# Spatial gate of the two late layers moved between the q and k projections and done in place, and the state output put back in channel order by ACT

## The chip, the cores and the metric

The kernel runs on one core of a Trainium2 chip. Its time is the device time of one execution in microseconds (us); the median of three runs of the kernel before is 2917.49 us (2912.63 to 2918.08). The engines are PE (TensorE, matmuls and transposes), DVE (VectorE), ACT (ScalarE), POOL (GpSimd) and SP (SyncE, which here only issues transfers). Each has its own instruction queue and works it off in order; they meet at semaphores.

## What is computed

The reference is a model of four layers at 512 tokens and width 1024, all in f32: an attention layer and a convolution layer with a mixture of experts, and then two "late" layers that this change is about. What a late layer does before its feed-forward part, cut to what matters:

```
def spatial_gating(u, v, v_gain, w_s, b_s):        # 256 channels, windows of 128 positions, 4 heads
    v = rms_norm_2(v, v_gain).reshape(bsz, nwin, GMLP_WINDOW, GMLP_HEADS, GMLP_HEAD_DIM)
    w = jnp.where(mask[None], w_s, 0)
    mixed = jnp.einsum("hij,bnjhc->bnihc", w, v) + b_s.T[None, None, :, :, None]
    return u * mixed.reshape(bsz, seq, GMLP_WIDTH)

xn = rms_norm_2(h, attn_norm_g[layer])
u_ssm, u_g, v_g, q, k, v = jnp.split(xn @ w_in[layer], [o1, o2, o3, o4, o5], axis=-1)
y_ssm = s5_mixer(u_ssm, ...)                       # complex diagonal state space model, 256 channels
y_sgu = spatial_gating(u_g, v_g, ...)
y_diff = diff_attention(q, k, v, ...)              # 4 heads, two softmax maps each, their difference on v
mixed = jnp.concatenate([y_ssm, y_sgu, y_diff], axis=-1)
h = h + mixed @ w_out[layer]
```

## The kernel before

The program is written by hand for each engine, and nothing is scheduled by a tool: what stands in a block (`block.tensor`, `block.vector`, `block.scalar`, `block.gpsimd`) runs in that order. Large products are done in three f32r matmuls per tile (L598 to L600: high times high, low times high, high times low), for which POOL splits each weight tile in two (L2024 rounds, L2026 takes the rest). PSUM has eight banks and every PE result takes the next one in turn (`claim`): a tile can begin only when the tile eight places before it was drained.

A late layer `l` (0 or 1; the code loops over `L2`) has these stages on PE.

- **In-projection.** u for the state space model (names `u`), then the 512 columns of the gate, `ugv` (u_g and v_g, token-major, 4 tiles), then the 512 columns of v, `vD`. ACT takes both out of PSUM (L1879). Then ACT computes the root mean square of v_g (L1883 to L1885), copies the turned gate weights (`wT`, L1887), and works out the exponentials of lambda.
- **The q/k stage.** `normed(groups2(l), ...)` runs over eight groups, q and k of head 0, q and k of head 1, and so on. In step i PE does the projection of group i (24 matmuls), the mean square of group i-1 (L800) and the rotation of group i-2 (L814). `between(i, end)` puts attention work between the groups from step 4 on.
- **The tail.** The last units of attention, the state space model and the gate, up to the out-projection `out2`. Attention has 16 units m = 4 x head + query tile. `attend(i)` does the scores of unit i+2 (PE L1287, DVE `maxima` L2918), the exponentials (ACT `probs` L1896), the ratio of the two maps (DVE L2926, L2927), its application (ACT L1905), the merging of the maps (POOL L2331), and for units i and i-1 the turning of the probabilities (PE L1295, ACT L1914) and their product with v (PE L1305, ACT `take_values` L1923, L1924). The state space model runs in two halves a: `state_in` (PE L1260), `turn_in` (DVE L2881), `scan` (DVE L2895), `turn_out` (DVE L2904 to L2907), `state_out` (PE L1271, L1274).

In the tail, before this change: `vn`, the normalised v_g, is written by DVE (L2978) after the last rotation, since its place in the arena is also that of a buffer of the rotations. PE multiplies it by the turned weights in `spatial_gate` (L1247), after `attend(7)`. DVE adds the bias and multiplies by u_g into `gate_out` (L2988) after `scan(0)`. `take_runs(a)` (DVE L2970) copies the state output of half a (key `yp`) from runs of 32 partitions back into channel order, in 16 copies of 32 partitions x 128 elements, each to columns 4 apart, after `attend(10)` and `attend(14)`. `TURN_AFTER` says after which `attend` PE turns the finished tiles of the out-projection's input (`turn_tile(k)`, L1327: k = 2, 3 the gate, 4 to 7 the heads); ACT rounds them (`round_late`, L1946) and DVE takes the rest (`rest_late`, L2945), after the same unit and after the next. POOL splits the first weights of `out2` two units at a time after `merge_maps(13)`, `(14)` and `(15)`.

Of the kernel before, what the change touches and what calls it, by code (L numbers as in the profile page):

```python
# [11 lines left out]
ALU = mybir.AluOpType  # L12
# [35 lines left out]
TURN_AFTER = {10: (4,), 11: (2, 3), 12: (5,), 15: (6,)}  # L48
# [88 lines left out]
def build(nc, A, out, upto=99):  # L137
    ctx = ExitStack()
    with ctx:
# [127 lines left out]
        gate_out = region(18688, 2, T)  # L267
# [28 lines left out]
        vn = region(21760, NT, 256)  # L296
# [247 lines left out]
        def _(pe):  # L544
# [680 lines left out]
            for l in range(L2):  # L1225
# [92 lines left out]
                def turn_tile(k):  # L1318

                    if k >= 4:  # L1320
                        pe.wait_ge(S("subln_done"), 4 * l + k - 3)
                    else:
                        wait_drained(pe, ("sgu", l, NT - 1))
                    ps = claim(("mt", l, k))
                    for t in range(NT):
                        src = gate_out[:, k - 2, t * P:(t + 1) * P] if k < 4 else qD[:, k - 4, t * P:(t + 1) * P]
                        ins = pe.transpose(ps[:, t * P:(t + 1) * P], src, c("ident"))  # L1327
                    fill(ins, ("mt", l, k))
# [9 lines left out]
                def between(i, end):  # L1338

                    if 4 <= i < 8:  # L1340
                        attend(2 * i - 9)
                    elif i == 8 and end:
                        attend(6)
# [7 lines left out]
                spatial_gate()  # L1351
                attend(8)
                state_in(1)
                attend(9)
                state_out(0)
                for m in range(10, UNITS_LATE + 1):
                    attend(m)
                    for k in TURN_AFTER.get(m, ()):
                        turn_tile(k)
                    if m == 13:  # L1360
                        state_out(1)
# [121 lines left out]
        def _(act):  # L1483
# [388 lines left out]
            for l in range(L2):  # L1872
                (norm_added if l else norm_results)(f"at{l}")
                act.wait_ge(S("rstd_ready"), SPLIT_NORMS.index(f"at{l}") + 1)
                for s, dst in ((f"ugv{l}", ugv), (f"vd{l}", vD)):
                    for t in range(NT):
                        key = ("dn", s, 0, t)
                        ps = wait_filled(act, key)
                        drain(act.activation(dst[:, t, :], ps[:, :], ACT.Copy, scale=rstd[:, t:t + 1]), key)  # L1879
                ln_exp_table()  # L1880
# [4 lines left out]
                act.activation(s5("rstd"), lnv, ACT.Exp, scale=-0.5).then_inc(S("v_rms"), 1)  # L1885
                ps = wait_filled(act, ("wt", l))
# [55 lines left out]

                def round_late(k):

                    ps = wait_filled(act, ("mt", l, k))
                    act.activation(mix_hi[:, k, :], ps[:, :], ACT.Copy).then_inc(S("rows_rounded"), 1)  # L1946
# [11 lines left out]
                for m in range(8, UNITS_LATE + 1):  # L1958
                    attend(m)
                    for k in TURN_AFTER.get(m, ()):  # L1960
                        round_late(k)
# [416 lines left out]
        def _(dve):  # L2378
# [465 lines left out]
            for l in range(L2):  # L2844
# [112 lines left out]
                def between(i, end):  # L2957

                    if 4 <= i < 8:
                        attend(2 * i - 10 + end)  # L2960
                    elif i == 8 and end:
                        attend(6)

                def take_runs(a):

                    key = ("yp", l, a)
                    ps = wait_filled(dve, key)
                    for k in range(4):
                        for s in range(RUN):
                            ins = dve.tensor_copy(yg[32 * k:32 * k + 32, a, s:T:RUN],  # L2970
                                                  ps[32 * s:32 * s + 32, k * P:(k + 1) * P])
                    drain(ins, key)

                normed2(l, rb, between)
                dve.wait_ge(S("v_rms"), l + 1)
                dve.wait_ge(S("rope_done"), 16 + 8 * (l + 1))
                for t in range(NT):
                    dve.scalar_tensor_tensor(out=vn[:, t, :], in0=ugv[:, t, 256:512], scalar=s5("rstd")[:, t:t + 1],  # L2978
                                             in1=vgain, op0=ALU.mult, op1=ALU.mult).then_inc(S("vn_ready"), 1)
                turn_in(0)  # L2980
                attend(7)
                scan(0)
                for t in range(NT):
                    ps = wait_filled(dve, ("sgu", l, t))
                    for h in range(4):
                        hs = slice(h * 64, (h + 1) * 64)
                        at = t * P + (h % 2) * 64
                        ins = dve.scalar_tensor_tensor(out=gate_out[:, h // 2, at:at + 64], in0=ps[:, hs],  # L2988
                                                       scalar=vcol("gmlp_b_s_2", 4 * l + h), in1=ugv[:, t, hs],
                                                       op0=ALU.add, op1=ALU.mult)  # L2990
                    drain(ins, ("sgu", l, t))
# [5 lines left out]
                for m in range(10, UNITS_LATE + 1):  # L2997
                    attend(m)
                    if m == 11:
                        turn_out(1)  # L3000
                    if m in (10, 14):
                        take_runs(m // 4 - 2)
                    for k in TURN_AFTER.get(m - 1, ()):
                        rest_late(k)
# [70 lines left out]
```

## Time and profile before

| | before |
|---|---|
| median of three runs | 2917.49 us |
| the profiled execution | 2922.09 us, of which the span is 2920.3 us |
| PE, DVE, ACT, POOL busy | 96%, 36%, 25%, 53% of the span |
| mean granted TensorE clock | 0.978 |

The span runs from the first to the last recorded instruction of that one execution; 1.8 us lie around it. The profiled execution is 4.6 us above the median. Times in the rows are from the start of the span. The q/k stage of layer 0 is 1755.86 to 1834.30, its tail 1834.30 to 1890.36; in layer 1 the same two are 2367.63 to 2445.99 and 2445.99 to 2502.57. A stage is taken from its first PE instruction to that of the next one.

### The profile page before, as it was taken

The page shows a single profiled execution, that of the slowest core. Times are in us where ns is not written, and L with a number is a line of the kernel's source. Part 1 is how long each engine was busy: PE and PEld are TensorE (multiplying, and loading weights), DVE is VectorE, ACT ScalarE, POOL GpSimd, SP SyncE. Part 2 cuts the span into 40 slices and gives each one's busy share as a digit, 9 for nine tenths or more (in the row PEclk, how much of TensorE's full clock was granted, in tenths as well). Part 3 has the DMA queues.
Part 4 walks back from the last instruction along what each step waited for, and adds up shares of the span by engine and source line. Part 5 has one row for each costly group of instructions (what it writes and reads, how often), then busy time and mean ns, then how long its engine had stood idle before and what let it go on. Part 6 is the DMA issues. An engine that isn't in the chain of part 4 may idle for free.

```text
span 2920.3 us, 38219 instructions
## 1 busy us (share of the span) xinstructions
PE 2803.0 (96%) x14585; PEld 2332.8 (80%) x14585; DVE 1053.3 (36%) x2141; ACT 722.4 (25%) x1799; POOL 1547.1 (53%) x1681
## 2 busy tenths in 40 slices
PE   7899999999999989999999989799999997999999
PEld 3545888888878889999999976678888775788887
DVE  1035652313235510000000233837356327466372
ACT  2135752101120101111111024532112234421020
POOL 2121027777777541322280255468888653588786
PEclk9998999999999979999999999899999998999999
DMA  8460013333253269899999930342332312332321
GB/s 189 101 173 15 16 30 87 97 98 101 83 170 101 59 182 277 246 264 254 258 259 263 274 94 16 120 114 85 110 87 88 100 44 91 101 101 94 101 85 52
DMA packets 540391, 371.25 MB, mean 127 GB/s; under 512 B 31489, under 2 KB 493128, under 8 KB 539307
## 3 DMA queue, kind: packets, MB, share of 16 engines
q1 hardware_dynamic: 522144, 321.58, 39.0%
q0 software_dynamic: 11472, 33.13, 3.6%
q10 hardware_dynamic: 6586, 14.03, 1.9%
q8 instruction: 119, 1.95, 0.3%
q14 instruction: 70, 0.57, 0.1%
HBM read 336.73 MB, written 32.41 MB: 126 GB/s over the span
## 4 chain that ended last, share of the span: by engine, by line
PE 87%; DVE 5%; issue 3%; ACT 2%; DMA 2%; POOL 1%; ACTq 0%; another core or an unknown queue 0%; DVEq 0%; SPq 0%; POOLq 0%
PE bank L598 18%; PE bank L600 18%; PE bank L599 18%; PE bank L758 15%; PE bank L1192 7%; PE bank L852 2%; PE bank L830 2%; DMA ring<-in_ev_w_in 1%; PE bank L840 1%; PE bank L800 1%; PE bank L814 1%; DMA ring<-in_moe_w_up 1%; ACT x_hi L1585 1%; PE bank L957 1%; DVE x L2565 1%
## 5 line engine op out<-in xcount | busy, mean ns | idle before, releaser
L2026 POOL TENSOR_TENSOR unit_parts<-ring,unit_parts 128x512 fp32r<-128x512 f32 x580 | 804.4, 1387 | 48.4
L2024 POOL TENSOR_SCALAR unit_parts<-ring 128x512 fp32r<-128x512 f32 x580 | 423.5, 730 | 488.5 <-PE bank L600 341.1
L598 PE MATMUL bank<-x_hi,unit_parts 128*128 128x512 f32 x1408 | 556.6, 395 | 19.3 <-DVE x L2565 10.3
L599 PE MATMUL bank<-x_lo,unit_parts 128*128 128x512 f32 x1408 | 551.0, 391 | 0.0
L600 PE MATMUL bank<-x_hi,unit_parts 128*128 128x512 f32 x1408 | 551.0, 391 | 0.0
L758 PE MATMUL bank<-arena,ring 128*128 128x160 f32 x2816 | 389.1, 301 | 4.6 <-ACT arena L1771 3.7
L758 PEld LDWEIGHTS bank<-arena,ring 128*128 128x128 f32 x2816 | 386.1, 191 | 5.8 <-ACT arena L1771 3.9
L598 PEld LDWEIGHTS bank<-x_hi,unit_parts 128*128 128x128 f32 x1408 | 266.5, 189 | 78.2 <-issue 11.7
L598 PE MATMUL bank<-unit_parts,hid_parts 128*128 128x512 f32 x784 | 308.3, 393 | 3.2 <-DVE hid_parts L2587 2.6
L599 PEld LDWEIGHTS bank<-x_lo,unit_parts 128*128 128x128 f32 x1408 | 266.2, 189 | 55.9 <-issue 1.4
L600 PEld LDWEIGHTS bank<-x_hi,unit_parts 128*128 128x128 f32 x1408 | 266.1, 189 | 55.9
L600 PE MATMUL bank<-unit_parts,hid_parts 128*128 128x512 f32 x784 | 305.5, 390 | 0.0
L599 PE MATMUL bank<-unit_parts,hid_parts 128*128 128x512 f32 x784 | 305.4, 390 | 0.0
L2633 DVE TENSOR_TENSOR arena<-bank,arena 128x160 f32<-128x160 f32 x88 | 28.6, 325 | 573.6 <-PE bank L758 569.2
L1192 PE MATMUL bank<-arena,ring 128*128 128x160 f32 x1408 | 193.4, 300 | 0.5 <-DVE arena L2633 0.5
L1192 PEld LDWEIGHTS bank<-arena,ring 128*128 128x128 f32 x1408 | 191.5, 190 | 1.0 <-DVE arena L2633 0.7
L1987 ACT ACTIVATE arena<-arena,vec 128x512 f32<-128x512 f32 x88 | 71.9, 817 | 464.4 <-DVE arena L3025 464.4
L2565 DVE TENSOR_TENSOR x<-bank,x 128x512 f32<-128x512 f32 x80 | 55.2, 691 | 335.5 <-PE bank L600 335.5
L598 PEld LDWEIGHTS bank<-unit_parts,hid_parts 128*128 128x128 f32 x784 | 147.5, 188 | 34.9 <-DVE hid_parts L2587 2.8
L600 PEld LDWEIGHTS bank<-unit_parts,hid_parts 128*128 128x128 f32 x784 | 147.3, 188 | 30.8
L599 PEld LDWEIGHTS bank<-unit_parts,hid_parts 128*128 128x128 f32 x784 | 147.4, 188 | 30.5 <-issue 0.5
L3029 DVE SCALAR_TENSOR_TENSOR arena<-arena,vec 128x511 f32<-128x511 f32 x88 | 78.7, 894 | 78.0 <-ACT arena L1987 78.0
(359 smaller groups left out, 3415.5 us busy)
## 6 DMA issues: line engine op xcount, KB each, us to landing
ring<-in_moe_w_gate SPq DMA_DIRECT2D x88, 512.0 KB, 5.9
ring<-in_moe_w_up SPq DMA_DIRECT2D x88, 512.0 KB, 7.1
ring<-in_moe_w_down SPq DMA_DIRECT2D x64, 704.0 KB, 5.0
ring<-in_w_up SPq DMA_DIRECT2D x88, 512.0 KB, 5.2
ring<-in_w_down SPq DMA_DIRECT2D x16, 1024.0 KB, 5.1
ring<-in_od_w_in SPq DMA_DIRECT2D x24, 512.0 KB, 4.6
ring<-in_ffn_w_gate SPq DMA_DIRECT2D x22, 512.0 KB, 4.0
ring<-in_ffn_w_up SPq DMA_DIRECT2D x22, 512.0 KB, 5.2
```

The costliest lines, as they stand in the source:

```text
L598: pe.matmul(ps, a[0], b[0], start=start, stop=False)
L599: pe.matmul(ps, a[0], b[1], start=False, stop=False)
L600: return pe.matmul(ps, a[1], b[0], start=False, stop=stop)
L758: ins = pe.matmul(ps[rows_at:rows_at + m, 0:n], w[:, k * width + at:k * width + at + m], src[:, k, :], start=k == 0, stop=k == KD - 1)
L830: ins = pe.matmul(ps[:, 0:k.shape[1]], u["q"](t), k, start=k is ks[0], stop=k is ks[-1])
L852: ins = pe.matmul(ps[:, 0:u["vw"]], pT_buf[0:w, j % 2, kt * P:kt * P + P], u["v"](kt, w), start=kt == 0, stop=kt == kts - 1)
L1192: ins = pe.matmul(ps[:, (m - m0) * CAP:(m - m0 + 1) * CAP], w[:, k * P:(k + 1) * P], hidE[:, k, :], start=k == 0, stop=k == KE - 1)
L1987: act.activation(acc[:, 2 * a + n % 2, :], unscaled[:, a, :], ACT.Identity, scale=vcol("conv_w_2", 132 * l + 88 + f), bias=vcol("conv_b_2" ...
L2024: pool.tensor_scalar(hi, raw, 1.0, 1.0, ALU.mult, ALU.mult).then_inc(S("units_rounded"), 1)
L2026: pool.tensor_tensor(lo, raw, hi.bitcast(F32), ALU.subtract).then_inc(S("units_split"), 1)
L2565: drain(dve.tensor_tensor(xs, ps[:, :], xs, ALU.add), key)
L3029: link(dve.scalar_tensor_tensor(out=o[:, 1:T], in0=b[:, 0:T - 1], scalar=vcol("conv_w_2", 132 * l + 44 + f), in1=o[:, 1:T], op0=ALU.mult, ...
```

## The change

In both late layers:

- `vn` gets a place in the two ring slots that are held for the attention maps. DVE writes it before the q/k stage and no longer waits for the rotations.
- PE does `spatial_gate` at the end of step 1 of the q/k stage, and DVE its part there too, in place: the product overwrites u_g in `ugv`, and `gate_out` is gone.
- ACT takes `ugv`, computes the root mean square of v_g, and only then takes `vD`.
- `take_runs` goes from DVE to ACT, after the same units.
- `TURN_AFTER`: tiles 2 and 3 are turned after unit 9 instead of 11, tile 4 after unit 11 instead of 10. ACT rounds tile 2 only when tile 3 has been turned too, since it writes where `ugv` stands. `state_out(0)` keeps its place.

```
-TURN_AFTER = {10: (4,), 11: (2, 3), 12: (5,), 15: (6,)}
+TURN_AFTER = {9: (2, 3), 11: (4,), 12: (5,), 15: (6,)}
-        vn = region(21760, NT, 256)
+        vn = held[:, 0:2, :].rearrange("p a (b n) -> p (a b) n", b=2)
 # PE
-                        src = gate_out[:, k - 2, t * P:(t + 1) * P] if k < 4 else qD[:, k - 4, t * P:(t + 1) * P]
+                        src = ugv[:, t, (k - 2) * P:(k - 1) * P] if k < 4 else qD[:, k - 4, t * P:(t + 1) * P]
-                    if 4 <= i < 8:
+                    if i == 1 and end:
+                        spatial_gate()
+                    elif 4 <= i < 8:
...
                 attend(7)
-                spatial_gate()
                 attend(8)
                 state_in(1)
-                attend(9)
-                state_out(0)
-                for m in range(10, UNITS_LATE + 1):
+                for m in range(9, UNITS_LATE + 1):
                     attend(m)
+                    if m == 9:
+                        state_out(0)
 # ACT
+                take_rows(f"ugv{l}", ugv)
                 ln_exp_table()
...
                 act.activation(s5("rstd"), lnv, ACT.Exp, scale=-0.5).then_inc(S("v_rms"), 1)
+                take_rows(f"vd{l}", vD)
...
+                def take_runs(a):
+                    key = ("yp", l, a)
+                    ps = wait_filled(act, key)
+                    for k in range(4):
+                        for s in range(RUN):
+                            ins = act.activation(yg[32 * k:32 * k + 32, a, s:T:RUN],
+                                                 ps[32 * s:32 * s + 32, k * P:(k + 1) * P], ACT.Copy)
+                    drain(ins, key)
                 def round_late(k):
+                    if k == 2:
+                        wait_filled(act, ("mt", l, 3))
...
                     attend(m)
+                    if m in (10, 14):
+                        take_runs(m // 4 - 2)
 # DVE
-                normed2(l, rb, between)
                 dve.wait_ge(S("v_rms"), l + 1)
-                dve.wait_ge(S("rope_done"), 16 + 8 * (l + 1))
                 for t in range(NT):
                     dve.scalar_tensor_tensor(out=vn[:, t, :], in0=ugv[:, t, 256:512], scalar=s5("rstd")[:, t:t + 1],
                                              in1=vgain, op0=ALU.mult, op1=ALU.mult).then_inc(S("vn_ready"), 1)
+                normed2(l, rb, between)
...
-                    if m in (10, 14):
-                        take_runs(m // 4 - 2)
```

The changed file has other line numbers: PE L1246 is before's L1247, L799 is L800, L1286, L1294, L1304 and L1326 are L1287, L1295, L1305 and L1327, L1270 and L1273 are L1271 and L1274; ACT L1900 to L1928 are L1896 to L1924, L1962 is L1946.

PE, layer 0, where the tail begins before: the last rotation (L814), `state_in(0)` (L1260), `attend(7)`, the gate (L1247), and `attend(8)`.

```order
L814 MATMUL bank<-arena,cst 128x512
L1260 MATMUL bank<-arena 128x128 x12
L1287 MATMUL bank<-arena 128x256 x2
L1295 MATMUL bank<-cst,ring 128x128 x4
L1305 MATMUL bank<-arena,ring 128x128 x3
L1247 MATMUL bank<-arena,wT_buf 128x64 x16
L1287 MATMUL bank<-arena 128x384 x2
```

PE of the changed kernel, layer 0, step 1 of the q/k stage: the end of the projection of k, the mean square of q, and behind it the gate, ahead of the projection of head 1.

```order
L598 MATMUL bank<-x_lo,unit_parts 128x512
L599 MATMUL bank<-x_hi,unit_parts 128x512
L799 MATMUL bank<-arena,cst 128x512
L1246 MATMUL bank<-ring,wT_buf 128x64 x16
L597 MATMUL bank<-x_hi,unit_parts 128x512
L598 MATMUL bank<-x_lo,unit_parts 128x512
```

The 16 matmuls of the gate are the same ones; they went from the tail to the q/k stage.

ACT before, tail of layer 0, from `scale_map(11)` (L1905) on: `attend(10)`, the rounding of tile 4, `attend(11)`, the rounding of tiles 2 and 3, and `attend(12)`.

```order
L1905 ACTIVATE ring<-ring,small 128x512
L1914 ACTIVATE ring<-bank 128x384
L1923 ACTIVATE arena<-bank,small 128x128
L1924 ACTIVATE cst,small<-bank,small 128x128
L1946 ACTIVATE hid_parts<-bank 128x512
L1896 ACTIVATE ring,small<-ring,small 128x256 x2
L1905 ACTIVATE ring<-ring,small 128x128
L1914 ACTIVATE ring<-bank 128x512
L1923 ACTIVATE arena<-bank,small 128x128
L1924 ACTIVATE cst,small<-bank,small 128x128
L1946 ACTIVATE hid_parts<-bank 128x512 x2
L1896 ACTIVATE ring,small<-ring,small 128x384 x2
```

ACT of the changed kernel at the same place.

```order
L1909 ACTIVATE ring<-ring,small 128x512
L1918 ACTIVATE ring<-bank 128x384
L1927 ACTIVATE arena<-bank,small 128x128
L1928 ACTIVATE cst,small<-bank,small 128x128
L1953 ACTIVATE arena<-bank 32x128 x16
L1900 ACTIVATE ring,small<-ring,small 128x256 x2
L1909 ACTIVATE ring<-ring,small 128x128
L1918 ACTIVATE ring<-bank 128x512
L1927 ACTIVATE arena<-bank,small 128x128
L1928 ACTIVATE cst,small<-bank,small 128x128
L1962 ACTIVATE hid_parts<-bank 128x512
L1900 ACTIVATE ring,small<-ring,small 128x384 x2
```

The 16 copies of `take_runs(0)` (L1953) stand between `attend(10)` and the exponentials of unit 13; tiles 2 and 3 are rounded earlier and tile 4 takes their place.

PE before, tail of layer 0, from the last two instructions of `state_out(0)` on: `attend(10)` (128x128 scores), tile 4, `attend(11)`, tiles 2 and 3.

```order
L1274 MATMUL bank<-xnT,arena 128x127 x2
L1274 MATMUL bank<-krT,arena 128x127
L1287 MATMUL bank<-arena 128x128 x2
L1295 MATMUL bank<-cst,ring 128x128 x3
L1305 MATMUL bank<-arena,ring 128x128 x2
L1327 MATMUL bank<-cst,arena 128x128 x4
L1287 MATMUL bank<-arena 128x256 x2
L1295 MATMUL bank<-cst,ring 128x128 x4
L1305 MATMUL bank<-arena,ring 128x128 x3
L1327 MATMUL bank<-cst,arena 128x128 x8
```

PE of the changed kernel at the same place.

```order
L1273 MATMUL bank<-xnT,arena 128x127 x2
L1273 MATMUL bank<-krT,arena 128x127
L1326 MATMUL bank<-cst,arena 128x128 x8
L1286 MATMUL bank<-arena 128x128 x2
L1294 MATMUL bank<-cst,ring 128x128 x3
L1304 MATMUL bank<-arena,ring 128x128 x2
L1286 MATMUL bank<-arena 128x256 x2
L1294 MATMUL bank<-cst,ring 128x128 x4
L1304 MATMUL bank<-arena,ring 128x128 x3
L1326 MATMUL bank<-cst,arena 128x128 x4
```

Tiles 2 and 3 stand ahead of `attend(10)`, and tile 4 after `attend(11)`. With `state_out(0)` counted as the first, the tile that takes its bank again, the eighth after it, was the turned probabilities of unit 11; in the changed kernel it is the second score of unit 13.

## Rows read from the trace of the kernel before

**Rows 1.** The page: the chain that ended last, share by engine

```profile
PE 87%; DVE 5%; issue 3%; ACT 2%; DMA 2%; POOL 1%; ACTq 0%; another core or an unknown queue 0%; DVEq 0%; SPq 0%; POOLq 0%
```

**Rows 2.** Windows by stage: window, length, busy times of each engine, granted clock, DMA

```profile
1755.86:1834.30 78.44, 73.03 (x302) 49.99 (x303) 36.29 (x90) 39.68 (x106) 40.54 (x42) 0.96 0.16 50
1834.30:1890.36 56.06, 41.47 (x271) 35.55 (x270) 52.56 (x138) 26.11 (x85) 27.57 (x27) 0.84 0.19 68
2367.63:2445.99 78.36, 73.69 (x303) 50.79 (x304) 36.29 (x90) 39.70 (x106) 40.50 (x42) 0.96 0.16 51
2445.99:2502.57 56.58, 40.24 (x272) 34.63 (x270) 53.24 (x139) 26.26 (x86) 27.57 (x27) 0.86 0.18 66
```

**Rows 3.** Timeline of DVE, tail of layer 0: start, length, instruction

```profile
1836.26 1.67 DVE L2978 SCALAR_TENSOR_TENSOR arena<-arena,s5small,cst 128x256 f32<-128x256 f32 x4
...
1845.00 3.13 DVE L2988 SCALAR_TENSOR_TENSOR arena<-bank,vec,arena 128x64 f32<-128x64 f32 x16
...
1861.77 6.27 DVE L2970 COPY arena<-bank 32x128 f32<-32x128 f32 x16
```

**Rows 4.** Timeline of PE, layer 0: start, length, instruction, idle before

```profile
1838.99 0.70 PE L1287 MATMUL bank<-arena 64*128 64x256 f32 x4
...
1840.78 3.68 PE L1247 MATMUL bank<-arena,wT_buf 128*128 128x64 f32 x32
1844.39 0.92 PE L1287 MATMUL bank<-arena 64*128 64x384 f32 x4
...
1868.10 1.11 PE L1295 MATMUL bank<-cst,ring 128*128 128x128 f32 x4 [6.18 <-DVE arena L2970]
...
1870.28 1.91 PE L1327 MATMUL bank<-cst,arena 128*128 128x128 f32 x8
...
1886.57 1.09 PE L1295 MATMUL bank<-cst,ring 128*128 128x128 f32 x4 [4.16 <-POOL ring L2331]
```

**Rows 5.** Timeline of ACT, tail of layer 0

```profile
1863.38 0.21 ACT L1924 ACTIVATION_READ_ACCUMULATOR cst<-bank,small 128x1 f32 x1
...
1884.83 0.21 ACT L1924 ACTIVATION_READ_ACCUMULATOR cst<-bank,small 128x1 f32 x1
1887.76 0.60 ACT L1914 ACTIVATE ring<-bank 128x512 f32<-128x512 f32 x1 [2.72 <-PE bank L1295]
```

**Rows 6.** Timeline of POOL, tail of layer 0

```profile
1875.70 0.73 POOL L2331 TENSOR_TENSOR ring<-ring 128x256 f32<-128x256 f32 x1 [5.00 <-ACT ring L1905]
...
1885.17 1.25 POOL L2331 TENSOR_TENSOR ring<-ring 128x512 f32<-128x512 f32 x1
```

**Rows 7.** Groups by form: xcount, busy us, mean ns, idle before

```profile
L2970 DVE COPY arena<-bank 32x128 f32<-32x128 f32 x64 | 24.5, 382 | 0.8
...
L1834 ACT ACTIVATE cst<-bank 32x128 f32<-32x128 f32 x4 | 1.1, 272 | 0.0
```

**Rows 8.** Timeline of ACT, layer 0: a contiguous copy and what follows it

```profile
1875.53 0.26 ACT L1914 ACTIVATE ring<-bank 128x128 f32<-128x128 f32 x1
1875.69 0.35 ACT L1923 ACTIVATE arena<-bank,small 128x128 f32<-128x128 f32 x1
```

**Rows 9.** Timeline, step 1 of the q/k stage of layer 0: PE, then DVE

```profile
1767.31 0.79 PE L598 MATMUL bank<-x_hi,unit_parts 128*128 128x512 f32 x1
...
1769.68 0.75 DVE L2512 SCALAR_TENSOR_TENSOR arena<-arena,vec 128x512 f32<-128x512 f32 x1 [1.94 <-ACT arena L1624]
1773.36 0.69 DVE L2497 TENSOR_TENSOR arena<-bank,arena 128x512 f32<-128x512 f32 x1 [2.93 <-PE bank L600]
```

**Rows 10.** Timeline of ACT ahead of the q/k stage, layer 0

```profile
1760.16 0.19 ACT L1889 ACTIVATE small<-small 128x2 f32<-128x2 f32 x1
```

**Rows 11.** Timeline, tail of layer 1: PE, then DVE

```profile
2448.76 0.70 PE L1287 MATMUL bank<-arena 64*128 64x256 f32 x4
...
2449.64 0.68 DVE L2881 TENSOR_TENSOR xnT<-bank,cst 128x512 f32<-128x512 f32 x1
...
2473.51 6.27 DVE L2970 COPY arena<-bank 32x128 f32<-32x128 f32 x16
```

More of the change, by code:

```diff
@@ L266, in build @@
         yg = region(21760, 2, T)
-        gate_out = region(18688, 2, T)
         held = ring[:, (SLOTS - HELD_SLOTS) * SLOT:SLOTS * SLOT].rearrange("p (a t) -> p a t", a=8)
@@ L1874, in _, with take_rows @@
                 act.wait_ge(S("rstd_ready"), SPLIT_NORMS.index(f"at{l}") + 1)
-                for s, dst in ((f"ugv{l}", ugv), (f"vd{l}", vD)):
+                def take_rows(s, dst):
                     for t in range(NT):
@@ L2957, in between @@
                 def between(i, end):
-                    if 4 <= i < 8:
+                    if i == 1 and end:
+                        spatial_gate()
+                    elif 4 <= i < 8:
                         attend(2 * i - 10 + end)
@@ L2962, in between, with spatial_gate @@
                         attend(6)
[L2964 to L2972, printed above, removed]
-                normed2(l, rb, between)
+                def spatial_gate():
+                    for t in range(NT):
+                        ps = wait_filled(dve, ("sgu", l, t))
+                        for h in range(4):
+                            hs = slice(h * 64, (h + 1) * 64)
+                            ins = dve.scalar_tensor_tensor(out=ugv[:, t, hs], in0=ps[:, hs],
+                                                           scalar=vcol("gmlp_b_s_2", 4 * l + h), in1=ugv[:, t, hs],
+                                                           op0=ALU.add, op1=ALU.mult)
+                        drain(ins, ("sgu", l, t))
                 dve.wait_ge(S("v_rms"), l + 1)
-                dve.wait_ge(S("rope_done"), 16 + 8 * (l + 1))
                 for t in range(NT):
@@ L2982, in _ @@
                 scan(0)
[L2983 to L2991, printed above, removed]
                 attend(8)
```

## Prediction

> **What bounds the kernel now.** The page comes first: the chain of work that ended last is 87% PE, 5% DVE and 2% ACT [rows 1], so other engines matter only where PE waits for them. The change touches only the two late layers, so the next view is the busy time by stage [rows 2]. In the q/k stage PE is busy 73.0 of 78.4 us, and DVE and ACT about half of it: that stage is bound by PE. In the tail PE is busy 41.5 of 56.1 us and DVE 52.6 of 56.1: up to its last third the tail is bound by DVE. Layer 1 shows the same two pictures (73.7 of 78.4; 40.2 and 53.2 of 56.6). A microsecond of PE work is thus worth a whole one in the q/k stage and little in the tail, and DVE work the other way round.
>
> The timelines of the tail say which waits count. DVE runs without a gap to the end of the 16 copies of `take_runs(0)`, at 1868.04 [rows 3], and PE then has waited 6.18 us with the turning of unit 11's maps, which needs the bank that these copies drain [rows 4]. The last wait of PE, 4.16 us, is for the merging of unit 15 on POOL [rows 4]. POOL does this 1885.17 to 1886.42, and began the merging of unit 13 at 1875.70 [rows 6]; between the two it has one more merging and the splitting of four weight units, back to back, so that these 10.7 us stay whatever DVE does.
>
> **The gate, on PE.** The 16 matmuls of one layer take from 1840.78 to 1844.39, 3.61 us [rows 4]. In the tail nothing is gained by their leaving: DVE reaches the scores behind them only after its own work on the gate, which ends at 1848.1 [rows 3]. In the q/k stage they stand between the mean square and the next projection, which follow each other without a wait [rows 9], so each layer pays 3.61 us, 7.2 in all. Nothing else should be late there: ACT now finishes the root mean square before `vD`, so that the turned weights come earlier than the 1760.16 at which ACT is through with all this now [rows 10]; DVE's gate work (3.13 us, [rows 3]) falls between the instruction that ends about 1770.4 and the next projection at 1773.4, which itself moves 3.6 us later [rows 9]. If that cover were gone, those 3.1 us a layer would be paid again.
>
> **vn and the gate, on DVE.** The tail loses 1.67 us of `vn` and 3.13 of the gate [rows 3]. In layer 0 the first is not gained: `turn_in(0)` needs the end of `state_in(0)`, and PE comes to its next instruction only at 1838.99 [rows 4], 2.7 us after `vn` starts, whereas `turn_in` without `vn` would need its third tile earlier. The granted clock is 0.84 over this tail [rows 2], so some of its matmuls ran at 1.2 GHz. In layer 1 `state_in(0)` ends by 2448.76 and `turn_in(0)` starts 2449.64 [rows 11], so `vn` counts there. DVE is then ahead by 3.13 us in layer 0 and 4.80 in layer 1 when it comes to unit 12. `vn` itself now runs before the projection of q is ready, beside POOL's splitting; no charge.
>
> **take_runs, on ACT.** This is the term that decides. DVE needs 6.27 us for 16 copies, 382 ns each [rows 3, 7]. No row shows ACT writing columns 4 apart. Nearest are its copies of 32x128 out of PSUM at changing partitions: 272 ns each [rows 7]. I take that, 4.35 us for 16. From below I bound it by a contiguous 128x128 copy, behind which the next instruction starts 0.16 us later [rows 8], 2.6 us for 16; from above by DVE's own 6.27 us.
>
> The Trainium skill, "ScalarE: Activation LUTs", § What ACT_TABLE_LOAD costs, gives 186 ns + 0.833 ns an element for an ACTIVATE without pointer operands, and lets successive ones overlap by 93 ns: an estimate of 0.20 us each. The row of 272 ns is close to its 293 without the overlap. By the page's overlapped figure the whole sum below would come to -3.5 us instead of +1.1.
>
> First block. ACT finishes unit 9's values at 1863.6 [rows 5]. With DVE 3.13 us ahead this is 1860.5, and the bank is drained at 1864.8 instead of 1868.0. It is another tile that waits for it now: the second score of unit 13 (about 0.3 us), ahead of the same turning of unit 11. So PE goes on 2.9 us earlier in layer 0, and 1.67 more, 4.6 us, in layer 1 (whose copies start at the same point of the tail, [rows 11]). Behind that PE turns one tile instead of two: half of 1.91 us [rows 4], 0.95. The merging of unit 13 starts 3.9 and 5.5 us earlier; POOL's 10.7 us follow, and the turning of unit 15 moves by as much.
>
> Second block. ACT finishes unit 13's values at 1885.04, and must copy the turned maps of unit 15 at 1887.76 [rows 5]: 2.72 us of room for 4.35 us of copies. What is late next is that copy, and PE's product behind it, by 1.6 us in each layer. On DVE the second block delayed nothing, so this is a new cost.
>
> Tail: -3.9 + 1.6 = -2.3 us in layer 0, -5.5 + 1.6 = -3.9 in layer 1, together -6.1 before rounding. With the 7.2 of the q/k stages the **sum is +1.1 us**. Moving ACT's `vD` copies, the in-place writes and the turning of tiles 2 and 3 one stage earlier cost nothing that I can find: they lie under DVE's `scan(1)` and `turn_in(1)`. Against the profiled 2922.1 us the sum is 2923.2; the median of the runs lies 4.6 lower, so 2918.6. The ends of the sum are a few tenths soft on the good side (waits between engines that vanish), and I say 2918.
>
> **The rivals.** (A) The forecast: what leaves the tail and what enters the q/k stage are about equal. Within 0.2% (5.8 us), which is about what a measurement of this kernel can tell from no change. Chance 0.55.
>
> (B) ACT's copies are cheap, at 0.16 us each. First block: bank drained at 1863.0, 4.7 and 6.4 us gained, with the tile 5.65 and 7.3; second block: 2.6 us fit into 2.72, no delay. Tail -13.0, sum -5.8: 2912. For it speaks that ACT's contiguous copies overlap so [rows 8]; against it that its 32-partition copies do not: they take 272 ns each [rows 7], more than the 0.26 us of the contiguous copy before its overlap, and they change partitions from one to the next as these do. The same side is reached if the gate's matmuls cost nothing in the q/k stage, since then 7.2 us fall away (-6.1, 2911); against it stand the back-to-back rows there. Chance of both 0.24.
>
> (C) Slower: ACT's copies cost what DVE's do, 0.39 us each, since they write columns 4 apart. First block gains 1.0 and 2.7, with the tile 1.95 and 3.6; the second is late by 3.55 in each. Tail +1.5, sum +8.7: 2926. It decides from where the sum passes +5.8: each tenth of a microsecond in the price is 6.4 us in the sum (64 copies), so from 0.345 us. For it speaks DVE's own row; against it that the 382 ns contain DVE's own start of an instruction, which I can't separate. Chance 0.21.
>
> The Trainium skill, "SBUF — State Buffer", § Door 1: The DMA port swizzle, speaks for (C): it says that SBUF keeps lines of 16 bytes and that accesses which step to a new line each time pay a penalty, and columns 4 apart in f32 are just that step. No row shows ACT doing it.
>
> That the change does not do what it says I exclude: the order of instructions shows both moves.
>
> **How the numbers follow.** The predicted time is that of (A). Its own range is 2913 to 2924; with parts of (B) and (C) the range that should hold 8 times in 10 is 2911 to 2926. Faster by over 0.2%: 0.24. Within 0.2%: 0.55. Slower by over 0.2%: 0.21.
>
> **What the profile would show.** The q/k stages should be 3.6 us longer each (82.0 us) and without a new wait; the tails 2.3 and 3.9 us shorter. The ACT copies should read about 272 ns. In the tail the wait of PE ahead of the second score of unit 13 should end with ACT's copies, not DVE's, about 2.9 us earlier from the tail's start than the wait of 6.18 us ends now. ACT's copy of unit 15's maps should follow its own copies directly, no longer a wait for PE. The merging of units 13 to 15 should again take 10.7 us. The prediction is wrong if the copies are far from 272 ns, if DVE's gate makes a projection or rotation late in the q/k stage, or if the attention chain behind `take_runs(0)` is held by something else, such as the state space model's first half.

## The result and the profile after

The change made the kernel slower. In twelve runs of each, on one chip, the median went from 2917.45 to 2927.68 us: a ratio of 1.0036, 95% interval 1.0027 to 1.0045, or +10.5 us (7.9 to 13.1). I had predicted 2918.

The windows by stage of the changed kernel are q/k stage and tail of layer 0, then of layer 1 (the kernel before in [rows 2]):

```profile
1751.30:1833.36 82.06, 77.04 (x334) 53.91 (x335) 43.77 (x110) 35.83 (x95) 41.01 (x42) 0.96 0.15 49
1833.36:1889.64 56.28, 35.71 (x240) 29.50 (x238) 36.45 (x87) 38.05 (x117) 27.85 (x27) 0.80 0.18 66
2368.02:2448.20 80.18, 75.53 (x334) 53.08 (x335) 43.75 (x110) 35.59 (x94) 40.98 (x42) 0.98 0.15 48
2448.20:2505.78 57.58, 36.70 (x239) 29.97 (x238) 36.51 (x87) 38.47 (x118) 27.83 (x27) 0.79 0.18 67
```

Against before the four differ by +3.62, +0.22, +1.82 and +1.00 us. PE's busy time left the tail (41.5 to 35.7 us) and DVE's too (52.6 to 36.5), and the tail is still not shorter. The stretches behind the tails, up to the next q/k stage and to the end of the span, are 1.1 us longer each, nearly all of it at the head of the out-projection (under "The clock" below); the part ahead of layer 0's q/k stage, where nothing was changed, happened to be 4.6 us shorter in this execution. Without that the two profiled executions differ by 8.9 us, and the runs by 10.5.

What the change has to do with it is one row of the groups by form (the kernel before in [rows 7]):

```profile
L1953 ACT ACTIVATE arena<-bank 32x128 f32<-32x128 f32 x64 | 24.8, 387 | 0.7
```

A copy takes ACT 387 ns, not 272: five more than DVE needed. PE's timeline of the changed kernel, layer 0 (the kernel before in [rows 4]):

```profile
1763.14 3.68 PE L1246 MATMUL bank<-ring,wT_buf 128*128 128x64 f32 x32
...
1833.36 2.93 PE L1259 MATMUL bank<-arena 128*128 128x128 f32 x24
...
1864.12 1.22 PE L1286 MATMUL bank<-arena 64*128 64x256 f32 x2 [9.61 <-ACT arena L1953]
...
1882.41 1.08 PE L1294 MATMUL bank<-cst,ring 128*128 128x128 f32 x4 [4.16 <-POOL ring L2349]
1883.29 1.49 PE L1304 MATMUL bank<-arena,ring 128*128 128x128 f32 x6
1884.57 1.06 PE L1326 MATMUL bank<-cst,arena 128*128 128x128 f32 x4
1887.94 2.05 PE L1304 MATMUL bank<-arena,ring 128*128 128x128 f32 x8 [2.31 <-ACT ring L1918]
1889.64 0.77 PE L597 MATMUL bank<-unit_parts,hid_parts 128*128 128x512 f32 x1
```

The gate's matmuls stand in the q/k stage. The wait for the bank of `state_out(0)` now ends with ACT, 30.76 us into the tail (before: 33.80). PE's wait for POOL ahead of unit 15's turning is 4.16 us as before. New is the last wait, 2.31 us for ACT ahead of the values of unit 15 (L1304). ACT's timeline says what ACT did meanwhile (the kernel before in [rows 5]):

```profile
1857.75 6.32 ACT L1953 ACTIVATE arena<-bank 32x128 f32<-32x128 f32 x16
...
1880.76 6.42 ACT L1953 ACTIVATE arena<-bank 32x128 f32<-32x128 f32 x16
1887.20 0.60 ACT L1918 ACTIVATE ring<-bank 128x512 f32<-128x512 f32 x1
```

The copy of unit 15's maps was ready to be made when PE had turned them (1883.5) and came behind the second block. The values themselves took 2.05 us, in before 1.06: the windows give a granted clock of 0.50 (1.2 GHz) from 1887.94 on in the changed kernel and of 1.00 (2.4 GHz) over the same matmuls before. The first row is of the changed kernel, the second, in its own fence, of the kernel before.

```profile
1887.94:1889.64 1.70, 1.70 (x9) 1.70 (x9) 0.65 (x1) 0.95 (x4) 0.00 (x0) 0.50 0.04 10
```

```profile
1889.55:1890.36 0.81, 0.81 (x10) 0.81 (x9) 0.03 (x1) 0.74 (x3) 0.75 (x1) 1.00 0.07 20
```

### The profile page after: what moved, and what is told of

It is laid out like the page before. It is cut to its first block, busy times and chain, and to the rows that moved or that the text cites. A ratio compares the mean times of both kernels' runs of the same rounds, so it can differ in the third digit from the quotient of the medians.

```text
span 2924.6 us, 38221 instructions
## 1 busy us (share of the span) xinstructions
PE 2795.1 (96%) x14585; PEld 2324.9 (79%) x14585; DVE 1034.3 (35%) x2077; ACT 746.1 (26%) x1863; POOL 1549.4 (53%) x1681
## 4 chain that ended last, share of the span: by engine, by line
PE 87%; DVE 4%; ACT 3%; issue 2%; DMA 2%; POOL 0%; ACTq 0%; another core or an unknown queue 0%; DVEq 0%; SPq 0%; POOLq 0%
PE bank L597 18%; PE bank L598 18%; PE bank L599 18%; PE bank L757 15%; PE bank L1191 7%; PE bank L851 2%; PE bank L829 2%; DMA ring<-in_ev_w_in 1%; PE bank L839 1%; PE bank L799 1%; PE bank L813 1%; ACT arena L1953 1%; DMA ring<-in_moe_w_up 1%; ACT x_hi L1585 1%; PE bank L956 1%
## 5 line engine op out<-in xcount | busy, mean ns | idle before, releaser
L1727 ACT ACTIVATE arena<-bank 128x160 f32<-128x160 f32 x88 | 26.8, 304 | 319.2 <-PE bank L757 311.7
```

## The experiments

All run on another chip than the result's, where the kernel before has a median of 2912.6 to 2912.7 us, so ratios are compared; 0.001 is 2.9 us. In the table, tails and q/k stages are of the profiled execution, layer 0 / layer 1. The ratio of the changed kernel is that of the result; its stages are compared across the two chips.

| kernel | ratio to before (95%) | q/k stages, us | tails, us |
|---|---|---|---|
| before | 1 | 78.44 / 78.36 | 56.06 / 56.58 |
| changed | 1.0036 (1.0027 to 1.0045) | 82.06 / 80.18 | 56.28 / 57.58 |
| runs_on_dve | 0.9994 (0.9985 to 1.0003) | 80.37 / 81.90 | 51.90 / 51.85 |
| runs_on_act | 1.0035 (1.0022 to 1.0047) | 76.82 / 76.67 | 60.95 / 60.68 |
| runs_flat | 1.0000 (0.9991 to 1.0009) | 80.45 / 80.46 | 52.42 / 54.45 |
| before_flat | 0.9990 (0.9981 to 0.9999) | 78.43 / 78.47 | 55.35 / 55.22 |
| second_split | 1.0034 (1.0021 to 1.0048) | 82.06 / 79.57 | 56.46 / 56.44 |
| both_dve_flat | 0.9995 (0.9986 to 1.0004) | 82.03 / 81.90 | 52.54 / 51.34 |
| split_early | 0.9963 (0.9949 to 0.9976) | 80.43 / 81.92 | 46.48 / 46.62 |
| gate_late | 1.0005 (0.9995 to 1.0015) | 76.75 / 78.43 | 58.15 / 56.18 |
| act_split_early | 1.0027 (1.0015 to 1.0038) | 82.02 / 80.21 | 56.32 / 55.03 |
| tiles_first | 0.9981 (0.9972 to 0.9990) | 80.26 / 82.05 | 50.41 / 51.84 |
| gate_kept | 0.9970 (0.9959 to 0.9981) | 78.43 / 75.93 | 51.28 / 51.10 |
| step_2 | one run, 2913.59 us | 80.42 / 79.55 | 52.62 / 52.71 |

**runs_on_dve: undo the second half of the change.**

```
 # from the changed kernel: ACT's take_runs and its calls go, and on DVE
+                    if m in (10, 14):
+                        take_runs(m // 4 - 2)
```

> The changed kernel with the 32 copies of take_runs of each layer given back to DVE, at their old places behind units 10 and 14; the gate stays between the q and k projections. Theory 1 (the price of ACT's copies and their place on ACT made the change slow): the gate costs 3.6 us in each q/k stage, DVE reaches take_runs(0) 3.1 us earlier in layer 0 and 4.8 in layer 1, one turning less stands behind it (0.95 each), and no second block is late: 7.2 - 4.05 - 5.75 = -2.6 us against the kernel before, about 2915, and no wait of PE for ACT ahead of the values of unit 15. Theory 2 (moving the gate is the loss whichever engine copies, since the tail does not hand on what DVE gains): the tails stay at 56 us and the q/k stages at 82, +7 against the kernel before, about 2925.

Theory 1 holds: -1.7 us, tails 4.2 and 4.7 shorter. The interval excludes theory 2's +7. DVE's timeline, layer 0:

```profile
1846.98 6.27 DVE L2978 COPY arena<-bank 32x128 f32<-32x128 f32 x16
```

That is 22.7 us into the tail; before it was 27.5 [rows 3]. All of gate and `vn` (4.7 of 4.8 us) is gained, in layer 0 too. The stages give a net gain of 3.4 us (tails -8.9, q/k stages +5.5); the runs show 1.7, with an interval that includes no change.

**runs_on_act: the other half alone.** The kernel before, with `take_runs` as the change writes it on ACT.

> The kernel before with nothing changed but take_runs moved to ACT, at the same places behind units 10 and 14; the gate stays in the tail. Theory 1 (price of the copies): each copy 386 ns; ACT starts the first block when it is through with unit 9's values and ends 6.2 us later, about 1.8 us later than DVE did; the second block pushes the copy of unit 15's maps by 3.5 us; 5.3 us a layer, +10.6 against the kernel before, about 2928. Theory 2 (the gate is the loss): the tails are about as before, within 2 us of 2917.5.

Theory 1 again: 1.0035, tails 4.9 and 4.1 longer. PE's timeline of layer 0 has both waits:

```profile
1865.13 1.11 PE L1295 MATMUL bank<-cst,ring 128*128 128x128 f32 x4 [7.94 <-ACT arena L1949]
...
1889.64 1.13 PE L1305 MATMUL bank<-arena,ring 128*128 128x128 f32 x8 [2.31 <-ACT ring L1914]
```

This half alone costs what the whole change costs; the other half (runs_on_dve) is worth about nothing.

**runs_flat: the changed kernel with contiguous copies on ACT.**

```
+        y_runs = region(10240, 2, T)
-                            ins = act.activation(yg[32 * k:32 * k + 32, a, s:T:RUN],
+                            ins = act.activation(y_runs[32 * k:32 * k + 32, a, s * P:(s + 1) * P],
...
-                    act.activation(yg[:, a, :], yg[:, a, :], ACT.Gelu_apprx_tanh)
+                    act.activation(yg[:, a, :].rearrange("p (j s) -> p j s", s=RUN),
+                                   y_runs[:, a, :].rearrange("p (s j) -> p j s", s=RUN),
+                                   ACT.Gelu_apprx_tanh)
```

> The changed kernel, the 64 copies on ACT write 128 contiguous columns into a free region (columns grouped by s), and the two Gelu activations of a layer read that region with a stride and write yg in token order. Theory 1 (the write stride of 4 columns makes a copy 386 ns instead of the 272 of the contiguous 32x128 copies): copies at about 272 ns, 1.8 us less for each block of 16; at 64 x 0.114 us = 7.3 us if all of it is on the path, against the changed kernel, so about 2920.5; the prediction's sum of +1.1 over the kernel before would then come out nearly. Theory 2 (an ACT copy that reads PSUM and changes partitions costs 386 ns in this row of copies, stride or not): copies at 386 ns and 2927.7 as the changed kernel.

Theory 1: 267 ns a copy, and the time of the kernel before. The row of the costliest groups, then the last wait of layer 0's tail in PE's timeline:

```profile
L1954 ACT ACTIVATE arena<-bank 32x128 f32<-32x128 f32 x64 | 17.1, 267 | 0.7
```

```profile
1883.93 1.13 PE L1305 MATMUL bank<-arena,ring 128*128 128x128 f32 x8 [0.34 <-ACT ring L1919]
1884.82 0.48 PE L598 MATMUL bank<-unit_parts,hid_parts 128*128 128x512 f32 x1
```

The new wait is 0.34 us instead of 2.31, and the values behind it run at full clock. By the ratios the stride was worth 10.5 us (3.6 thousandths, each ratio uncertain by 0.9), by the two tails 3.9 + 3.1 = 7.0; expected were 7.3. Twelve of the 16 copies of a block write other partitions than they read; at 267 ns on the mean this costs nothing over the near row's 272, so it is not what made them dear.

**before_flat: the same on DVE, gate where it was.**

> The kernel before with its 64 copies on DVE writing contiguous columns into a free region, and the Gelu activations reading it with a stride. If DVE pays for the stride as well: copies fall from 382 ns to between 200 and 300, the first block of 16 ends 1.3 to 2.9 us earlier and PE goes on that much earlier in both layers: 2.6 to 5.8 us under the kernel before, 2912 to 2915. If DVE's 382 ns are its own start and the reading of 128 columns out of PSUM: copies at 382 ns and the time of the kernel before, 2917.5. The strided reading by Gelu comes in the projection behind the tail, where PE does not wait for it: no cost expected.

DVE pays for the stride as well, 96 ns a copy. Of the 6.1 us of 64 copies the ratio shows about half (2.9 us, uncertain by 2.6). PE waits for the first block alone, and gets its bank 1.5 us earlier in layer 0 and 1.6 in layer 1:

```profile
L2973 DVE COPY arena<-bank 32x128 f32<-32x128 f32 x64 | 18.3, 286 | 0.8
```

**step_2: which stride costs.** Columns land in another order here, so this kernel computes something else than the reference and serves for the durations alone. It is the changed kernel with `yg[32 * k:32 * k + 32, a, s // 2 * 2 * P + s % 2:(s // 2 + 1) * 2 * P:2]` as the copies' output.

> The changed kernel with ACT's copies writing every second column instead of every fourth; columns land in another order, so the state output's time order is changed by this run. Theory (each step to a new 16-byte line costs): half as many new lines, about (267 + 387) / 2 = 327 ns a copy. Rival (any stride costs the same): 387 ns. Rival (steps of two columns are free): 267 ns.

```profile
L1953 ACT ACTIVATE arena<-bank 32x128 f32<-32x128 f32 x64 | 17.6, 275 | 0.7
```

275 ns: my half-way figure was wrong, two columns' step is nearly free (+8 ns) and four columns' costs +120. The Trainium skill, "Advanced Engine Details and Errata", § Memory Cachelines, says that a line of SBUF holds 16 bytes and that at least two accesses must hit a line to hide its latency. The three durations agree: with f32 a step of 2 leaves two hits, a step of 4 one. The run has a second use: it differs from the changed kernel in nothing but the step (Gelu reads as before), and its tails are 3.7 and 4.9 us shorter. So the gain of runs_flat is not from its rearranged Gelu.

**second_split: is ACT's second block a loss of its own?**

```
+                    if i == 14:            # between scale_map(15) and copy_turned(14)
+                        take_runs(1, range(2))
...
                     if m == 14:
+                        take_runs(1, range(2, 4))
```

> The changed kernel with ACT's second block of 16 strided copies cut in two: 8 go ahead of the copy of unit 14's turned maps (where ACT waits for the merging of unit 14 on POOL), 8 stay behind unit 13's values. The price of a copy is not touched. Theory (the second block was a new wait of its own, 2.3 us ahead of the values of unit 15 in each layer): that wait goes, PE's copy of unit 14's maps is at most slightly late, 4.6 us less than the changed kernel, +5.6 over the kernel before (ratio 1.0019). Rival (that wait only moves: ACT's eight copies of 3.1 us make the values of unit 14 late by as much): no change against the changed kernel, ratio 1.0035.

The rival holds: 1.0034. ACT's timeline shows why the gap that I meant to fill isn't there:

```profile
1872.75 0.72 ACT L1909 ACTIVATE ring<-ring,small 128x512 f32<-128x512 f32 x1 [3.11 <-DVE small L2950]
1873.38 3.21 ACT L1955 ACTIVATE arena<-bank 32x128 f32<-32x128 f32 x8
1876.60 0.49 ACT L1918 ACTIVATE ring<-bank 128x384 f32<-128x384 f32 x1
...
1877.72 3.19 ACT L1955 ACTIVATE arena<-bank 32x128 f32<-32x128 f32 x8
1880.94 0.60 ACT L1918 ACTIVATE ring<-bank 128x512 f32<-128x512 f32 x1
```

ACT's room, 3.11 us, lies ahead of `scale_map(15)`, not behind it; eight copies behind it push unit 14's maps, and PE's wait ahead of unit 15's values is 1.97 in layer 0 and 1.98 in layer 1.

**both_dve_flat: early gate, contiguous copies on DVE.**

> The gate between the q and k projections as in the changed kernel, the 64 copies on DVE and contiguous (286 ns instead of 382). If the bank behind take_runs(0) is what holds the tail in both layers, 16 x 0.096 = 1.5 us less for each layer than with the strided copies on DVE (ratio 0.9994): 3.1 us, ratio 0.9983. If with the gate gone something else holds the tail, no gain over 0.9994.

0.9995, with 0.9983 outside the interval. The copies are 1.5 us shorter a block, but the tail is shorter by 0.5 us in layer 1 alone; in layer 0 `state_in(0)` ran at the lower clock in this execution (4.81 us, runs_on_dve 2.84), which more than took it back. In layer 1 PE got the bank 1.50 us earlier (27.67 us into the tail, 29.17 in runs_on_dve) and the tail ended 0.51 earlier: two stretches behind the bank, up to the merging of unit 13 and from the turning of unit 15 on, are 0.5 us longer each, at a lower granted clock (0.83 over the tail, 0.87 in runs_on_dve). Layer 0:

```profile
1831.03 4.81 PE L1260 MATMUL bank<-arena 128*128 128x128 f32 x24
```

**split_early: what the freed place allows.** `gate_out` lay where two of the buffers for split weights lie, so POOL had to wait for its turning. In place, the gate frees them.

```
                     merge_maps(m)
-                    if m >= 13:
-                        wait_filled(pool, ("mt", l, 3))
-                        split(f"out2_{l}", 2)
+                    split(f"out2_{l}", {11: 3, 12: 2}.get(m, 0))
```

> As the one with contiguous copies on DVE and the early gate, and POOL splits five of the output projection's weight units behind the merging of units 11 (three) and 12 (two), where it waited 7.3 and 4.3 us, instead of four between the mergings of units 13 to 15. The old gate output shared its place with these buffers and the in-place gate freed it; POOL's wait for the turned gate tiles goes with it. Theory (the 10.7 us from the merging of unit 13 to the end of that of unit 15 are POOL's and set the end of the tail): 4 x 1.9 = 7.6 us at most come out of each tail, some 5 after the softmax chain of units 14 and 15 has become the bound: 10 us, ratio 0.995. Rival (the mergings wait for the softmax chain on DVE and ACT anyway, POOL's splitting only filled that time): no gain over the kernel with the late splitting, ratio 0.998.

The theory holds: 6.1 and 4.7 us out of the tails against both_dve_flat, 0.9963, the fastest kernel of this study (2899.95 us against 2912.68). POOL's mergings, layer 0:

```profile
1865.54 0.72 POOL L2340 TENSOR_TENSOR ring<-ring 128x256 f32<-128x256 f32 x1
1868.81 1.00 POOL L2340 TENSOR_TENSOR ring<-ring 128x384 f32<-128x384 f32 x1 [2.55 <-ACT ring L1910]
1870.66 1.26 POOL L2340 TENSOR_TENSOR ring<-ring 128x512 f32<-128x512 f32 x1 [0.85 <-ACT ring L1910]
```

Units 13 to 15 take 6.4 us instead of the 10.7 that I held to be fixed [rows 6], and POOL waits for ACT.

**act_split_early: the same edit on the changed kernel.**

> The changed kernel (strided copies on ACT, gate early), and nothing altered but POOL's splitting of weight units: five behind the mergings of units 11 and 12 instead of four between those of units 13 to 15. With contiguous copies on DVE the early splitting took 5 us out of each tail. Theory: the mergings come earlier, but ACT's second block of 6.2 us now stands wholly in the chain ahead of the copy of unit 15's maps, since PE's wait for POOL that covered most of it is gone: the wait for ACT grows from 2.3 to some 5 us, and only 2 us a layer are gained: ratio 1.002. Rival (ACT's block moves earlier by as much as the mergings do): 5 us a layer gained, ratio 1.000.

The theory holds: 1.0027. Layer 1's tail is 2.6 us shorter than the changed kernel's; layer 0's is not, but there `state_in(0)` took 4.6 us in this execution instead of 2.9. ACT's second block is now the bound, and its wait grew (layer 0; 5.04 us in layer 1):

```profile
1862.12 1.22 PE L1286 MATMUL bank<-arena 64*128 64x256 f32 x2 [9.86 <-ACT arena L1953]
...
1884.24 2.05 PE L1304 MATMUL bank<-arena,ring 128*128 128x128 f32 x8 [5.27 <-ACT ring L1918]
```

**gate_late: the gate behind unit 12.**

> As the one with the early splitting, but the 16 matmuls of the gate and DVE's work on it stand behind unit 12 in the tail, the turning of the gate's tiles behind unit 13, those of the first attention tiles behind unit 14; vn is written in place. Theory (in the q/k stage the matmuls cost their 3.6 us in full, and late in the tail PE and DVE have room): 3.6 us less in each layer than the early gate with the early splitting, ratio 0.9925. Rival (DVE's 3.1 us and the four banks stand in the chain of units 13 to 15, which the early splitting has just made the bound): the tails grow by what the q/k stages lose, ratio 0.995.

Worse than either: 1.0005. The q/k stages are 3.7 and 3.5 us shorter than split_early's, as the theory says, but the tails 11.7 and 9.6 longer. Two parts of that can be named. The 16 matmuls, 3.6 us in the q/k stage, take nearly twice that at a granted clock of 0.50:

```profile
1862.31:1869.17 6.86, 6.86 (x34) 6.74 (x33) 2.58 (x12) 1.66 (x7) 2.36 (x3) 0.50 0.00 0
```

Behind them, DVE's remainders of the turned tiles stand after its 16 copies, and PE waits 3.52 us for a bank. The rest I have not taken apart; over these tails the granted clock is 0.77, against 0.89 in split_early.

**tiles_first: turn the gate's tiles behind unit 8.**

> As the one with the early splitting (contiguous copies on DVE, gate early), but the two tiles of the gate are turned behind unit 8, before the state output takes its bank, so that the ninth tile behind that bank is no longer the second score of unit 13 but the values of unit 10. Theory (PE's 6.6 us for this bank are on the path only by what stands behind it, score, turning and unit 13's softmax): 1.2 us of scores and 1.1 of turning pass in the wait, 1 to 2 us a layer less, ratio 0.9955. Rival (DVE is the bound up to the end of its copies and takes the scores of unit 13 only behind them): no change, ratio 0.9963.

Both missed: 0.9981, slower than split_early by 4 to 5 us a tail. The bank that now comes late is that of a turned tile, which DVE drains behind `turn_in(1)` and unit 11's maxima (PE, layer 0):

```profile
1848.03 0.79 PE L1305 MATMUL bank<-arena,ring 128*128 128x128 f32 x2 [5.58 <-DVE hid_parts L2954]
```

**gate_kept: early splitting with the gate in its old place, in place.**

> As the one with the early splitting, but the gate's matmuls and DVE's work on them are back at their old place in the tail, behind the first half of the state space model; the gate is written in place all the same, vn is made ahead of the q and k projections, in place, and the tiles are turned behind unit 9. Theory (in place is what the change is good for, the move to the q/k stage is not): 3.6 us less in each q/k stage, DVE's 3.1 us back in each tail, 0.5 us a layer less or no difference: ratio 0.9960. Rival (the early gate is worth its place, since DVE's part there is covered): ratio 0.998 or more.

0.9970: its interval (0.9959 to 0.9981) overlaps split_early's, and it contains the theory's 0.9960 as well as the rival's 0.998. The q/k stages give back 2.0 and 6.0 us (the matmuls are 3.6; the second pair also differs in granted clock), the tails take 4.8 and 4.5. Early or late in the same kernel, the gate's place makes no difference that these runs tell.

## Why the prediction was wrong

**The failed step is the price of a copy on ACT.** "Nearest are its copies of 32x128 out of PSUM at changing partitions: 272 ns each [rows 7]. I take that". Size, source and type were matched, the write stride was not, and it is worth 120 of 387 ns (runs_flat against the changed kernel). The rows of DVE's 382 ns held the answer: 96 of them are the same stride, which I put down to "DVE's own start of an instruction". With 267 ns in place of 387 the kernel comes to 1.0000: the +1.1 of the sum, 0.4 thousandths, lies within runs_flat's interval of 0.9 to either side. Rival (C) had the price and its reason right, and the total (2926, +8.7) inside the measured interval, though some terms of it were off in ways that cancel (below); I gave it 0.21 because a near row looked safer than a matching stride.

**What of the sum held.** The q/k stages: +3.61 forecast, +3.62 in layer 0. In layer 1 the pair shows +1.82, at a granted clock of 0.98 against 0.96; over all profiled executions those with the early gate have a mean of 80.99 us (18 stages) and those without of 77.67 (10 stages), +3.3. DVE's gate work there was covered: it ran 1765.78 to 1768.93, and DVE then waited 3.47 us for the next projection.

The tails are the other way about: the sum had -2.3 and -3.9 us, measured were +0.2 and +1.0. Ahead of unit 15's turning 3.2 us were gained in layer 0 and 1.6 in layer 1, of the 3.9 and 5.5 forecast. That layer 0 comes near is luck: the dearer copies cost its first block 1.85 us, and `vn`'s 1.67, which the sum had left out there, made up for it. From the turning of unit 15 to the tail's end it is 7.23 us instead of 3.79 in layer 0, +3.4, and 7.21 instead of 4.58 in layer 1, +2.6. The working of (C) gives 3.55 for this, and that agreement is luck too: only 2.31 us of the 3.4 are the wait for ACT, and 0.99 are a lower clock that no sum contained. The copy of unit 15's maps is indeed 3.6 us late, but PE has the values of unit 14 and a tile to turn meanwhile. For the same reason the forecast's own 1.6 us was too much: in runs_flat, with copies of 267 ns, the stretch is 4.45 us, +0.7.

**What of it was off besides.** `vn`'s 1.67 us in layer 0 were "not gained" in the forecast, since `state_in(0)` took 4.7 us there. Over the 28 late layers profiled here it took 2.8 to 3.0 us in 20 and 4.2 to 4.9 in 8, in kernels of either order: a matter of the execution, on which no term should rest. Where it is short, `vn` is gained (runs_on_dve, 4.7 us ahead). "Turning one tile instead of two", 0.95 us, was not: from the freeing of the bank to the turning of unit 15 it is 18.29 us instead of 18.47, for the second score of unit 13, 1.15 us to the next instruction, stands there in its place; the sum had about 0.3 for it. The errors on `vn` and on the tile have opposite signs. That "these 10.7 us stay whatever DVE does" was true of this change and wrong of the kernel: it was an order of work that the change had made unnecessary (split_early).

**The clock, a cost that the sum did not have.** In layer 0 of the changed kernel the values of unit 15 took 0.99 us more than before, since they ran at 0.50, and the out-projection behind them began at the same level. These are its first 3.66 us, in the changed kernel and in the kernel before:

```profile
1889.64:1893.30 3.66, 3.66 (x14) 2.96 (x14) 1.19 (x5) 3.18 (x8) 0.00 (x0) 0.74 0.50 156
```

```profile
1890.36:1894.02 3.66, 3.66 (x19) 3.05 (x18) 1.83 (x5) 3.28 (x8) 0.50 (x1) 1.00 0.54 165
```

PE is busy throughout in both, with 14 matmuls in one and 19 in the other. The first 60 take 15.86 us instead of 14.94, and 16.59 instead of 15.54 in layer 1: 0.9 and 1.05 of the 1.1 us by which the stretch behind each tail grew. It goes with the wait for ACT. Eight of the 28 late layers profiled have a wait for ACT of 1.97 us or more ahead of unit 15's values (the changed kernel, runs_on_act, second_split, act_split_early), and there the 60 matmuls take 15.8 to 16.6 us; of the other 20 layers, 18 need 14.9 to 15.0, and one each of the kernel before and of gate_late 15.5 and 15.9. The wait doesn't begin the stretch at 0.50, it goes with a longer one: before, it lasts from 1886.1 to 1889.5; in the changed kernel from 1881.3, in PE's wait for POOL, over the wait for ACT to 1891.6. In runs_on_act it ends at 1887.5, the values run at 1.00 (1.13 us) behind the same wait of 2.31 us, and the lower level comes back from 1890.9 to 1894.4 (16.54 us for the 60). That the wait costs these microseconds is thus likely, but no run changes the wait alone, and why the level falls where it does stays open.

**Open.** The ratios put the stride at 10.5 us, the tails at 7.0. The first 60 matmuls of the out-projection add 0.9 and 1.65 us (15.86 and 16.59 against runs_flat's 14.93 and 14.94), which makes 9.6; the ratios are too uncertain to settle the remainder. Apart from this, late in the stretch between the two layers runs_flat and step_2 lose 1.3 to 1.4 us against the kernel before, and split_early gains as much; I have no cause for that.

## What to carry to other kernels

When you price an operation on another engine from a row of that engine, match the access pattern before the shape: a contiguous row doesn't price a write with a stride of four f32, on ACT or on DVE. If the data must be permuted, write contiguously and let one large instruction that comes later anyway read with the stride (here two Gelu activations, 1.04 us longer together), or keep two neighbouring f32 columns together (275 ns a copy, step_2). A late wait of PE can come with more than its own length: the one of 2.31 us in layer 0 came with a lower clock behind it, worth another 1.9 us in the changed kernel and 1.7 in runs_on_act. When a buffer becomes free, look for the wait that protected it: here that wait and the order of work that it had imposed, not the work moved, held the gain.

## What the hardware showed unexpectedly

- A 32x128 f32 copy from PSUM to SBUF on ACT: 267 ns contiguous, 275 with every second column, 387 with every fourth. On DVE 286 contiguous and 382 with every fourth. In blocks of 16 ACT starts one each 278 ns (4.45 us for 16) or 401 ns (6.42): no overlap beyond what the duration shows. The Trainium skill, "ScalarE: Activation LUTs", § What ACT_TABLE_LOAD costs, lets successive ACTIVATEs overlap by 93 ns; these copies, which change partitions each time, show none. A 128x128 copy of this case does overlap, by 0.10 us (0.26 us long, the next one starts after 0.16, [rows 8]); what makes the difference no run shows.
- Reading with a stride costs ACT more an element: two Gelu activations of 128x512 take 1.15 us contiguous (the kernel before) and 2.19 when they read a column 128 further on each time (before_flat, the row below), about 1.0 ns an element more. PE's waits in the 43 us behind the tail are the same in both, 0.3 us.

```profile
1884.15 2.19 ACT L1965 ACTIVATE arena<-arena 128x512 f32<-128x512 f32 x2
```
